# Seven products over 14 of 16 row tiles in the HGRN projections of a hybrid decoder step, with one weight sum on GpSimd

## The chip, the cores and the metric

The kernel runs on one core of a Trainium2 chip. The metric is the device time of one execution in microseconds (us). The kernel before takes 2852.39 us, the median of three runs (2851.09 to 2854.86).

## The reference

Two layers, the first RWKV-7, the second HGRN2, run over 512 prompt tokens and 8 x 4 sample tokens, 544 columns in all, with a model width of 2048. Everything is float32. The part that matters here is the input projection of the HGRN2 layer and the chunked recurrence that uses it:

```python
def hgrn2_mix(x, S_prev, lb, w_in, norm_w, w_o):
    q, f_logit, i, z = jnp.split(x @ w_in, 4, axis=-1)      # w_in: 2048 x 8192
    f = lb + (1.0 - lb) * jax.nn.sigmoid(f_logit)
    log_f = jnp.log(jnp.maximum(f, GATE_FLOOR))
    k = (1.0 - lb) * jax.nn.sigmoid(-f_logit)
    q = jax.nn.silu(q.astype(f32)) * HGRN_DK ** -0.5
    ...
    # per chunk: A = q k' with decays, o = A v + (q exp(G)) S, S = exp(G_last) S + k' v
    ...
    o = o * lax.rsqrt(jnp.mean(o * o, axis=-1, keepdims=True) + NORM_EPS) * norm_w
    out = (o.reshape(B, T, D).astype(x.dtype) * jax.nn.silu(z)) @ w_o
```

There are 16 heads of 128 channels; each head has four output tiles of 128 channels, for f, q, i (the values) and z (the gate).

## The kernel before

Activations are kept transposed: 16 row tiles (kt) of 128 channels by 544 tokens. A product in float32 accuracy is made of three TensorE passes over high and low parts: w_hi x_hi, w_hi x_lo and w_lo x_hi. ScalarE rounds a weight tile to its high part (a CAST), VectorE subtracts to get the low part. One pass over one half of the tokens is a matmul of 128x128 weights with 272 columns. A weight tile of 128 output channels, done plainly (function dense_kt), takes 16 row tiles x 2 token halves x 3 passes = 96 matmuls.

The HGRN tiles from number 20 to 75 are done in 28 pairs by a Strassen scheme with seven products in place of eight. A block is the pair's two output tiles times two row tiles times the two token halves. `U` counts the blocks along the rows. At U = 6 they take 12 of the 16 row tiles; the other 4 (`rest`, CW = 512 columns of the weight tile) are done plainly. One call of seven_products(q) is called a half here. It consists of eleven stretches, in this order: product 0, product 1, rest, rest, products 2, 3, 4, 5, rest, product 6, rest. A product is U x 3 matmuls, a rest is 4 x 3. After each three matmuls a counter goes up by one, and at certain counts a piece of the recurrence of the running or the last head is put between (`steps`): the level matmuls level(e, n) that build A, the outputs, the norm.

A head e from 1 to 14 has two halves: gates_pair (q even: it makes f and q of head e, and finishes head e-1) and values_pair (q odd: it makes v and z, and runs the levels of head e). Seven operands (items) of a half come from the two raw weight tiles raw[0] and raw[1]. Items 0, 1 and 6 are columns of the raw tiles. Items 2 to 5 are sums of them: S1 = raw1a + raw1b (weight_sum_1), S2 = S1 - raw0a (weight_sum_2), S3 = raw0a - raw1a (weight_sum_3), and S2 again = raw0b - S2 (weight_sum_4), which becomes item 5. All four sums stand on VectorE. Each item is then cast by ScalarE (item_hi) into one of three slots, and subtracted by VectorE (item_lo). VectorE also does the decays (widen), the copies of A (take), the states' chain (chain), the bank additions and the norms.

The order of the work on each engine is the order in which the code is written: gates_pair and values_pair exist once for ScalarE and once for VectorE, and the steps' counts set where TensorE does the recurrence. An engine does its list strictly in order, so an instruction that waits holds all that is behind it. The waits are:

- Level 0 waits for K and qr, level 1 for `first_q` (Q = qr * F, semaphore q1), and level n from 2 on for the widening before it (kx, qx).
- outputs(e, 0) waits for S[0] of `chain(e)`, outputs(e, 2) for S[2].
- The first matmul of product k waits for item_lo(q, k).
- GpSimd does the row sums of the activations once, before the pairs (row_sums), and then one product with the old sample states (t_Sd) and one masked copy (t_Vm) for each head.

Before the pairs, `scaled_rows`, `row_sums`, `sums_hi`, `sums_lo`, `third_sum_hi` and `third_sum_lo` make the seven combinations of the activations, once for each block j of the U.

Of the kernel before, what the change touches and what calls it, by code (L numbers as in the profile page):

```python
# [1392 lines left out]
def trunk(nc, keep, d):  # L1393

    with ExitStack() as ctx:
# [542 lines left out]
        def _(act):  # L1938
# [369 lines left out]
        def _(dve):  # L2308
# [18 lines left out]
            def weight_sum_1(q):  # L2327
                dve.wait_ge(raw_in[1], 16 * ((GS + 2 * q) // 2))
                if q:
                    dve.wait_ge(s.it_hi, ITEMS * (q - 1) + 4)  # L2330
                    dve.wait_ge(s.it_lo, ITEMS * (q - 1) + 4)
                dve.tensor_tensor(S1[:, :], raw[1][:, 0:UW], raw[1][:, UW:2 * UW], ALU.add).then_inc(s.s1, 1)

            def weight_sum_2(q):
                dve.wait_ge(raw_in[0], 16 * ((GS + 2 * q) // 2))
# [4 lines left out]
                else:  # L2340
                    dve.wait_ge(s.tile_ready, GS)
                dve.tensor_tensor(S2[:, :], S1[:, :], raw[0][:, 0:UW], ALU.subtract).then_inc(s.s2, 1)

            def weight_sum_3(q):
                if q:
                    dve.wait_ge(s.it_hi, ITEMS * (q - 1) + 5)
                    dve.wait_ge(s.it_lo, ITEMS * (q - 1) + 5)
# [513 lines left out]
```

## Time and profile before

| | us |
|---|---|
| median of three runs | 2852.39 |
| the profiled execution's own time | 2853.62 |
| its span, first to last instruction | 2851.8 |
| TensorE busy | 2730.1 (96%) |
| VectorE busy | 1608.9 (56%) |
| ScalarE busy | 1259.1 (44%) |
| GpSimd busy | 138.4 (5%) |

The page names engines PE (TensorE matmuls), PEld (its weight loads), DVE (VectorE), ACT (ScalarE), POOL (GpSimd) and SP (which issues DMAs). The pairs run from 1747.9 to 2562.8 us of the span. One head with its two halves takes 58.3 us. Matmuls are pipelined, so their recorded durations overlap: the time that one costs is the distance between starts. Durations of VectorE instructions overlap a little too.

### The profile page before, as it was taken

The page shows a single profiled execution, that of the slowest core. Times are in us where ns is not written, and L with a number is a line of the kernel's source. Part 1 is how long each engine was busy: PE and PEld are TensorE (multiplying, and loading weights), DVE is VectorE, ACT ScalarE, POOL GpSimd, SP SyncE. Part 2 cuts the span into 40 slices and gives each one's busy share as a digit, 9 for nine tenths or more (in the row PEclk, how much of TensorE's full clock was granted, in tenths as well). Part 3 has the DMA queues.
Part 4 walks back from the last instruction along what each step waited for, and adds up shares of the span by engine and source line. Part 5 has one row for each costly group of instructions (what it writes and reads, how often), then busy time and mean ns, then how long its engine had stood idle before and what let it go on. Part 6 is the DMA issues. An engine that isn't in the chain of part 4 may idle for free. (4 is left out here: it accounts for less than half of the span.)

```text
span 2851.8 us, 82517 instructions
## 1 busy us (share of the span) xinstructions
PE 2730.1 (96%) x36816; PEld 2567.6 (90%) x36816; DVE 1608.9 (56%) x2679; ACT 1259.1 (44%) x1869; POOL 138.4 (5%) x116
## 2 busy tenths in 40 slices
PE   6999999999999999999889988999999999999997
PEld 5899999999998887888779978999999999999997
DVE  7335313313326777888742267776777767775224
ACT  5345323324414555555532255444544455444222
POOL 0000000000001111010000003000000000000000
PEclk8999999999999999999999999999999999999999
DMA  3333333333311111112132242222333223243322
GB/s 126 108 106 113 109 113 113 113 111 134 115 69 52 50 53 54 51 53 71 43 111 89 90 155 73 95 95 94 97 100 107 95 80 114 95 139 137 124 89 102
DMA packets 86816, 273.48 MB, mean 96 GB/s; under 512 B 16448, under 2 KB 29504, under 8 KB 65984
## 3 DMA queue, kind: packets, MB, share of 16 engines
q1 hardware_dynamic: 77248, 250.37, 26.5%
q10 hardware_dynamic: 9216, 17.83, 1.7%
q8 instruction: 292, 4.78, 0.7%
q14 instruction: 60, 0.49, 0.1%
HBM read 221.63 MB, written 46.54 MB: 94 GB/s over the span
## 5 line engine op out<-in xcount | busy, mean ns | idle before, releaser
L136 PE MATMUL w_pair<-a_x_hi,keep_w_hi 128*128 128x272 f32 x2016 | 428.4, 294 | 19.3 <-DVE a_x_lo L1059 18.5
L136 PE MATMUL w_pair<-a_x_lo,keep_w_hi 128*128 128x272 f32 x2016 | 419.7, 289 | 0.0
L136 PE MATMUL w_pair<-a_x_hi,keep_w_lo 128*128 128x272 f32 x2016 | 417.4, 288 | 0.0
L1045 DVE TENSOR_TENSOR keep_w_lo<-keep_raw,keep_w_hi 128x2048 fp32r<-128x2048 f32 x63 | 144.4, 2293 | 469.5 <-ACT keep_w_hi L798 469.5
L136 PEld LDWEIGHTS w_pair<-a_x_hi,keep_w_hi 128*128 128x128 f32 x2016 | 320.2, 189 | 25.7 <-issue 20.7
L136 PEld LDWEIGHTS w_pair<-a_x_lo,keep_w_hi 128*128 128x128 f32 x2016 | 318.1, 189 | 0.0
L136 PEld LDWEIGHTS w_pair<-a_x_hi,keep_w_lo 128*128 128x128 f32 x2016 | 317.8, 189 | 0.0
L136 PE MATMUL t_pair<-t_x_hi,keep_w_hi 128*128 128x272 f32 x1216 | 262.0, 297 | 18.2 <-DVE t_x_lo L2421 9.1
L136 PE MATMUL t_pair<-t_x_lo,keep_w_hi 128*128 128x272 f32 x1216 | 253.5, 290 | 0.0
L136 PE MATMUL t_pair<-t_x_hi,keep_w_lo 128*128 128x272 f32 x1216 | 253.3, 290 | 0.0
L812 ACT ACTIVATE a_stage<-w_pair 128x544 f32<-128x544 f32 x64 | 40.0, 625 | 425.1 <-PE w_pair L136 425.1
L136 PEld LDWEIGHTS t_pair<-t_x_hi,keep_w_hi 128*128 128x128 f32 x1216 | 192.3, 190 | 27.8 <-issue 11.8
L1657 PE MATMUL t_pair<-t_x_hi,u_it_hi 128*128 128x272 f32 x672 | 201.4, 300 | 0.0
L136 PEld LDWEIGHTS t_pair<-t_x_lo,keep_w_hi 128*128 128x128 f32 x1216 | 194.2, 191 | 0.0
L1657 PE MATMUL t_pair<-t_x_hi,u_it_lo 128*128 128x272 f32 x672 | 193.5, 288 | 0.0
L1657 PE MATMUL t_pair<-t_x_lo,u_it_hi 128*128 128x272 f32 x672 | 193.5, 288 | 0.0
L136 PEld LDWEIGHTS t_pair<-t_x_hi,keep_w_lo 128*128 128x128 f32 x1216 | 192.5, 190 | 0.0
L1657 PE MATMUL t_pair<-u_To,u_it_hi 128*128 128x272 f32 x896 | 185.5, 300 | 0.0
L1657 PEld LDWEIGHTS t_pair<-u_To,u_it_hi 128*128 128x128 f32 x896 | 140.6, 189 | 13.8 <-issue 10.6
L1657 PE MATMUL t_pair<-t_x_hi,u_c_hi 128*128 128x272 f32 x448 | 137.2, 306 | 0.0
L2314 DVE TENSOR_TENSOR keep_w_lo<-keep_raw,keep_w_hi 128x2048 fp32r<-128x2048 f32 x38 | 87.7, 2307 | 84.4 <-ACT keep_w_hi L1948 84.4
L798 ACT CAST keep_w_hi<-keep_raw 128x2048 fp32r<-128x2048 f32 x63 | 120.2, 1908 | 30.5 <-ACT a_stage L812 28.0
(448 smaller groups left out, 6146.7 us busy)
## 6 DMA issues: line engine op xcount, KB each, us to landing
keep_raw<-in_w_in SPq DMA_DIRECT2D x64, 1024.0 KB, 5.0
keep_raw<-in_hgrn_in SPq DMA_DIRECT2D x64, 1024.0 KB, 5.1
keep_raw<-in_rwkv_wo SPq DMA_DIRECT2D x16, 1024.0 KB, 5.0
keep_raw<-in_hgrn_wo SPq DMA_DIRECT2D x16, 1024.0 KB, 5.0
t_Ss<-in_hgrn_s SPq DMA_DIRECT2D x16, 512.0 KB, 7.1
out_hgrn_s<-t_Sd SPq DMA_DIRECT2D x16, 512.0 KB, 8.5
scr_r<-a_stage ACTq DMA_DIRECT2D x16, 272.0 KB, 2.2
scr_k<-a_stage ACTq DMA_DIRECT2D x16, 272.0 KB, 2.1
```

The lines of the kernel that those rows point to most:

```text
L136: mm = pe.matmul(out[:, a, 0:TH], w, x[:, kt, a * TH:(a + 1) * TH], start=(kt == order[0] and n == 0), stop=(kt == order[-1] and n == 2))
L798: act.copy(w_hi[2 if n == 2 else n % 2][:, :], raw[n % 2][:, :]).then_inc(p.raw_hi, 1)
L812: act.activation(halves(stage[n % 2][:, :]), pair[3 if n == 2 else n % 2][:, :, 0:TH], func).then_inc(p.evac, 1)
L1045: dve.tensor_tensor(w_lo[b][:, :], raw[n % 2][:, :], w_hi[b][:, :].bitcast(F32), ALU.subtract).then_inc(p.raw_lo, 1)
L1657: mm = pe.matmul(out, a, b, start=start and m == 0, stop=(m == 2), skip_group_check=True)
L2314: dve.tensor_tensor(w_lo[g % 2][:, :], raw[g % 2][:, :], w_hi[g % 2][:, :].bitcast(F32), ALU.subtract).then_inc(s.raw_lo, 1)
```

## The change

- U goes from 6 to 7, so the seven products cover 14 of 16 row tiles: items are 896 columns wide and no longer 768, and the rest is 256 columns and no longer 512. A block j = 6 is added to the sums made before the pairs.
- S1 has no tile of its own: weight_sum_1 writes over raw1a. weight_sum_3, which reads raw1a, therefore has to come first, and the order of the sums is 3, 1, 2, one behind the other. In values_pair they stand together before first_q; at the end of values_pair they stand together for the next half.
- weight_sum_4 goes from VectorE to GpSimd, which does it for both halves of a head before the head's t_Sd.
- ScalarE's k_copy(e-1) comes before item_hi(q, 2) in gates_pair.
- TensorE's wait for t_lo moves from before product 0 to before product 2 of the first half; the last item has another slot, with a wait for it_lo before it; a few tiles are laid elsewhere.

```diff
-U = 6
+U = 7
...
+        S1 = raw[1][:, 0:UW]
...
                 if q == 0:
                     pe.wait_ge(s.evac, GS - 1)
-                    pe.wait_ge(s.t_lo, 2 * U)
...
+                if q == 0:
+                    pe.wait_ge(s.t_lo, 2 * U)
                 product(2, X, False)
...
# ScalarE
             def gates_pair(e, q):
+                if e > 1:
+                    k_copy(e - 1)
                 item_hi(q, 2)
                 if e > 1:
                     act.wait_ge(s.evac, H0 + 4 * e)
                     act.wait_ge(s.q1s, q)
                     silu(zs, s.zs)
-                    k_copy(e - 1)
...
                 if e == 0:
                     sums_hi(4)
                     sums_hi(5)
+                    scaled_rows(6)
...
                 k_copy(e)
                 if e < KT - 1:
-                    for j in range(U):
+                    for j in range(U - 1):
                         third_sum_hi(j)
+                    sums_hi(U - 1)
+                    third_sum_hi(U - 1)
# GpSimd
+            def weight_sum_4(q):
+                pool.wait_ge(s.it_hi, ITEMS * q + 3)
+                pool.wait_ge(s.it_lo, ITEMS * q + 3)
+                pool.tensor_tensor(S2[:, :], raw[0][:, UW:2 * UW], S2[:, :], ALU.subtract).then_inc(s.s4, 1)
...
             for e in range(KT):
+                if 1 <= e < KT - 1:
+                    weight_sum_4(2 * e - 2)
+                    weight_sum_4(2 * e - 1)
# VectorE
+            def weight_sum_1(q):
+                dve.wait_ge(s.s3, q + 1)
+                dve.tensor_tensor(S1, S1, raw[1][:, UW:2 * UW], ALU.add).then_inc(s.s1, 1)
...
             def gates_pair(e, q):
                 if q:
                     lower_first(q - 1, zs)
-                weight_sum_3(q)
                 item_lo(q, 2)
-                weight_sum_4(q)
                 item_lo(q, 3)
                 if e > 1:
                     chain(e - 1)
...
             def values_pair(e, q):
                 lower_first(q - 1, qr)
+                weight_sum_3(q)
                 weight_sum_1(q)
+                weight_sum_2(q)
                 first_q(e)
-                weight_sum_2(q)
                 item_lo(q, 2)
                 item_lo(q, 3)
                 take(e, 0)
                 widen(e, 0)
-                weight_sum_3(q)
-                weight_sum_4(q)
                 item_lo(q, 4)
...
                 lower_second(q, zs)
                 if q < NQ - 1:
+                    weight_sum_3(q + 1)
                     weight_sum_1(q + 1)
                     weight_sum_2(q + 1)
```

First, the order of VectorE at the start of an odd half, before. t_wS1 is S1, u3_wS2 is S2, u3_wS3 is S3, it_lo and it_hi are an item's parts, and t_Q<-t_qr,t_F is first_q.

```order
L2382 TENSOR_TENSOR t_qr<-t_pair0,t_rstd2 128x272
L2332 TENSOR_TENSOR t_wS1<-keep_raw1 128x768
L2478 TENSOR_TENSOR t_Q<-t_qr,t_F 128x544
L2342 TENSOR_TENSOR u3_wS2_22008<-t_wS1,keep_raw0 128x768
L2320 TENSOR_TENSOR u0_it_lo_22003<-u3_wS2_22008,u0_it_hi_22002 128x768
L2320 TENSOR_TENSOR u2_it_lo_22005<-t_wS1,u2_it_hi_22004 128x768
```

The same place in the changed kernel, where keep_raw1<-keep_raw1 is S1 written in place:

```order
L2396 TENSOR_TENSOR t_qr<-t_pair0,t_rstd2 128x272
L2356 TENSOR_TENSOR u3_wS3_22009<-keep_raw0,keep_raw1 128x896
L2360 TENSOR_TENSOR keep_raw1<-keep_raw1 128x896
L2367 TENSOR_TENSOR u3_wS2_22008<-keep_raw1,keep_raw0 128x896
L2492 TENSOR_TENSOR t_Q<-t_qr,t_F 128x544
L2341 TENSOR_TENSOR u0_it_lo_22003<-u3_wS2_22008,u0_it_hi_22002 128x896
L2341 TENSOR_TENSOR u2_it_lo_22005<-keep_raw1,u2_it_hi_22004 128x896
```

first_q had one sum ahead of it and now has three.

Second, VectorE around the start of an even half, before; t_S0 to t_S3 are the chain of the last head.

```order
L2378 TENSOR_TENSOR t_zs<-t_zs,t_rstd2 128x272
L2332 TENSOR_TENSOR t_wS1<-keep_raw1 128x768
L2342 TENSOR_TENSOR u3_wS2_22008<-t_wS1,keep_raw0 128x768
L2382 TENSOR_TENSOR t_zs<-t_pair0,t_rstd2 128x272
L2348 TENSOR_TENSOR u3_wS3_22009<-keep_raw0,keep_raw1 128x768
L2320 TENSOR_TENSOR u2_it_lo_22005<-u3_wS2_22008,u2_it_hi_22004 128x768
L2353 TENSOR_TENSOR u3_wS2_22008<-keep_raw0,u3_wS2_22008 128x768
L2320 TENSOR_TENSOR u1_it_lo_22007<-t_wS1,u1_it_hi_22006 128x768
L2526 COPY t_S0<-t_tok 128x128
```

And the same place in the changed kernel:

```order
L2392 TENSOR_TENSOR t_zs<-t_zs,t_rstd2 128x272
L2356 TENSOR_TENSOR u3_wS3_22009<-keep_raw0,keep_raw1 128x896
L2360 TENSOR_TENSOR keep_raw1<-keep_raw1 128x896
L2367 TENSOR_TENSOR u3_wS2_22008<-keep_raw1,keep_raw0 128x896
L2396 TENSOR_TENSOR t_zs<-t_pair0,t_rstd2 128x272
L2341 TENSOR_TENSOR u2_it_lo_22005<-u3_wS2_22008,u2_it_hi_22004 128x896
L2341 TENSOR_TENSOR u1_it_lo_22007<-keep_raw1,u1_it_hi_22006 128x896
L2542 COPY t_S0<-t_tok 128x128
```

Sum 3 is now ahead of sum 2, and sum 4 is gone from between the two low parts.

Third, GpSimd over one head in the changed kernel; before, only the second and third rows stood there.

```order
L2307 TENSOR_TENSOR u3_wS2_22008<-keep_raw0,u3_wS2_22008 128x896 x2
L2319 TENSOR_TENSOR t_Sd<-t_Ss,t_E4 128x1024
L2324 TENSOR_TENSOR t_Vm<-t_vtok,t_k_h_seq 64x512
```

The two sums of weights are one for each half of the head.

## Rows read from the trace of the kernel before

**Rows 1.** The page, busy time by engine: us (share of the span) x instructions.
```profile
PE 2730.1 (96%) x36816; PEld 2567.6 (90%) x36816; DVE 1608.9 (56%) x2679; ACT 1259.1 (44%) x1869; POOL 138.4 (5%) x116
```
**Rows 2.** PE's waits, 1747 to 2582 us: us in total, times, longest.
```profile
PE t_tok L1818 <- ACT t_ktok L2098: 1.5, 1, 1.5
PE t_lev L1828 <- DVE t_S L2526: 1.1, 1, 1.1
PE t_pair L136 <- DVE t_zs L2382: 0.6, 1, 0.6
```
**Rows 3.** The chain in order of time: start, us, what, matmuls.
```profile
1999.12 14.72 PE t_pair L1657 x117
```
**Rows 4.** Busy time in one odd and one even half.
```profile
2009.54:2037.44 27.90, 27.90 (x407) 25.97 (x405) 25.94 (x56) 12.82 (x24) 2.19 (x2) 1.00 0.34 118
2037.44:2067.87 30.43, 30.29 (x232) 28.25 (x231) 17.84 (x28) 16.26 (x26) 1.22 (x1) 1.00 0.26 79
```
**Rows 5.** DVE, timeline of the odd half: start, us, instruction.
```profile
2011.30 0.43 DVE L2382 TENSOR_TENSOR t_qr<-t_pair,t_rstd 128x272 f32<-128x272 f32 x1
2011.65 0.95 DVE L2332 TENSOR_TENSOR t_wS<-keep_raw 128x768 f32<-128x768 f32 x1
2012.51 0.72 DVE L2478 TENSOR_TENSOR t_Q<-t_qr,t_F 128x544 f32<-128x544 f32 x1
...
2016.02 0.96 DVE L2320 TENSOR_TENSOR u_it_lo<-t_wS,u_it_hi 128x768 fp32r<-128x768 f32 x1
...
2017.54 0.42 DVE L2500 TENSOR_TENSOR t_Q<-t_Q,t_F 128x272 f32<-128x272 f32 x1
```
**Rows 6.** PE, timeline of the odd half: levels 1 and 2.
```profile
2015.53 0.46 PE L1777 MATMUL t_lev<-t_Q,t_K 128*32 128x32 f32 x32
...
2019.93 0.46 PE L1777 MATMUL t_lev<-t_Q,t_K 128*32 128x32 f32 x32
```
**Rows 7.** DVE, timeline around the start of the even half at 2037.44.
```profile
2036.82 0.95 DVE L2332 TENSOR_TENSOR t_wS<-keep_raw 128x768 f32<-128x768 f32 x1
2037.86 1.62 DVE L2342 TENSOR_TENSOR u_wS<-t_wS,keep_raw 128x768 f32<-128x768 f32 x1
...
2040.62 0.95 DVE L2320 TENSOR_TENSOR u_it_lo<-u_wS,u_it_hi 128x768 fp32r<-128x768 f32 x1
...
2042.58 0.96 DVE L2320 TENSOR_TENSOR u_it_lo<-t_wS,u_it_hi 128x768 fp32r<-128x768 f32 x1
2043.46 0.28 DVE L2526 COPY t_S<-t_tok 128x128 f32<-128x128 f32 x1
```
**Rows 8.** ACT, the same place.
```profile
2039.51 0.83 ACT L1960 CAST u_it_hi<-u_wS 128x768 fp32r<-128x768 f32 x1 [2.45 <-DVE u_wS L2342]
2040.25 0.65 ACT L2068 ACTIVATE t_zs<-t_zs 128x544 f32<-128x544 f32 x1
...
2041.71 0.84 ACT L1960 CAST u_it_hi<-t_wS 128x768 fp32r<-128x768 f32 x1
```
**Rows 9.** PE, the same half: the outputs of the last head.
```profile
2044.45 0.61 PE L1828 MATMUL t_lev<-t_A,t_vtok 128*128 128x128 f32 x4
```
**Rows 10.** POOL's timeline, one head.
```profile
2022.33 1.90 POOL L2298 TENSOR_TENSOR t_Sd<-t_Ss,t_E 128x1024 f32<-128x1024 f32 x1 [41.98 <-DVE t_E L2502]
2037.14 1.52 POOL L2303 TENSOR_TENSOR t_Vm<-t_vtok,t_k_h_seq 64x512 f32<-64x512 f32 x1 [12.92 <-ACT t_vtok L2093]
```
**Rows 11.** DVE, two instructions of one form in that head.
```profile
2022.53 2.24 DVE L2324 TENSOR_TENSOR u_c_lo<-keep_raw,u_c_hi 128x512 fp32r<-128x512 f32 x1
...
2029.86 0.69 DVE L2324 TENSOR_TENSOR u_c_lo<-keep_raw,u_c_hi 128x512 fp32r<-128x512 f32 x1
```
**Rows 12.** L2303 and L2284 by themselves: ns min/median/max, first and last start.
```profile
L2303 POOL TENSOR_TENSOR t_Vm<-t_vtok,t_k_h_seq x16: 1033/1522/1747, 1756.0 to 2623.1; 64x512 f32<-64x512 f32 x16
...
L2284 POOL TENSOR_TENSOR t_Ss<-t_zs,t_acc x2: 771/772/772, 1700.2 to 1724.4; 128x272 f32<-128x272 f32 x2
```
**Rows 13.** PE's waits before the pairs, 1703 to 1748 us.
```profile
PE t_lev L1785 <- DVE t_Q L2500: 2.8, 1, 2.8
```
**Rows 14.** Busy time behind the wait of 2.8 us; PEclk is the granted clock's share.
```profile
1735.50:1739.40 3.90, 3.61 (x28) 3.31 (x28) 3.90 (x9) 0.59 (x2) 2.00 (x2) 0.56 0.00 0
```

More of the change, by code:

```diff
@@ L1403, in trunk @@
         raw, w_hi, w_lo, o = keep.raw, keep.w_hi, keep.w_lo, keep.o
-        acc, rstd, rstd2, warm = sb("acc", [P, T]), sb("rstd", [P, T]), sb("rstd2", [P, T]), sb("warm", [P, 1])
+        acc, rstd_at = sb("acc", [P, T]), nc.sbuf_base
+        rstd, rstd2, warm = sb("rstd", [P, T]), sb("rstd2", [P, T]), sb("warm", [P, 1])
         lb, oml = sb("lb", [P, KT]), sb("oml", [P, KT])
@@ L1409, in trunk @@
         vtok, ktok = sb("vtok", [P, 5, P]), sb("ktok", [P, 5, P])
+        S_at = nc.sbuf_base
         S = [sb(f"S{c}", [P, P]) for c in range(4)]
@@ L1423, in trunk @@
         Tl = Area(nc, "u7", keep.lora_at).sb("Tl", [P, 2, 2, TH], F32R)
-        T42 = [Tl[:, 0:2], To[:, 0:2], To[:, 2:4], To[:, 4:6], To[:, 6:8], To[:, 9:11]]
-        T1 = [To[:, i] for i in (12, 13, 14, 15, 8, 11)]
+        Tm, Tr = sb("Tm", [P, 2, 2, TH], F32R), Area(nc, "u8", rstd_at).sb("Tr", [P, 2, TH], F32R)
+        T42 = [Tl[:, 0:2], To[:, 0:2], To[:, 2:4], To[:, 4:6], To[:, 6:8], To[:, 9:11], To[:, 12:14]]
+        T1 = [Tr, To[:, 14], To[:, 15], To[:, 8], To[:, 11], Tm[:, 0], Tm[:, 1]]
         T3_raw = [t[:, :, :].rearrange("p b v -> p (b v)")[:, TH * i:TH * i + TH] for t in (Ss, Sd) for i in range(3)]
+        T3_raw.append(Area(nc, "u9", S_at).sb("T3s", [P, TH])[:, :])
         squares = [sq, rs]
@@ L1468, in item_source @@
         def item_source(k):
-            return (raw[0][:, 0:UW], raw[0][:, UW:2 * UW], S2[:, :], S1[:, :], S3[:, :], S2[:, :], raw[1][:, UW:2 * UW])[k]
+            return (raw[0][:, 0:UW], raw[0][:, UW:2 * UW], S2[:, :], S1, S3[:, :], S2[:, :], raw[1][:, UW:2 * UW])[k]
         def weight_tile(g):
@@ L1959, in item_hi @@
                     act.wait_ge(s.tile_ready, GS - 1 if n < 2 else GS)
+                if (q, k) == (NQ - 1, ITEMS - 1):
+                    act.wait_ge(s.it_lo, n)
                 act.copy(item_slot(q, k)[0][:, :], item_source(k)).then_inc(s.it_hi, 1)
@@ L1991, in sums_hi @@
                 act.wait_ge(s.t_sum, 4 * j + 4)
+                if j in (3, 4):
+                    act.wait_ge(s.t_in, 2 * j + 4)
                 act.copy(T1[j][:, 0], even[:, half(0)]).then_inc(s.t_hi, 1)
@@ L2325, in rest_lo, with weight_sum_3 @@
                                   ).then_inc(s.c_lo, 1)
-            def weight_sum_1(q):
+            def weight_sum_3(q):
+                dve.wait_ge(raw_in[0], 16 * ((GS + 2 * q) // 2))
                 dve.wait_ge(raw_in[1], 16 * ((GS + 2 * q) // 2))
                 if q:
-                    dve.wait_ge(s.it_hi, ITEMS * (q - 1) + 4)
-                    dve.wait_ge(s.it_lo, ITEMS * (q - 1) + 4)
-                dve.tensor_tensor(S1[:, :], raw[1][:, 0:UW], raw[1][:, UW:2 * UW], ALU.add).then_inc(s.s1, 1)
+                    dve.wait_ge(s.it_hi, ITEMS * (q - 1) + 5)
+                    dve.wait_ge(s.it_lo, ITEMS * (q - 1) + 5)
+                else:
+                    dve.wait_ge(s.tile_ready, GS)
+                dve.tensor_tensor(S3[:, :], raw[0][:, 0:UW], S1, ALU.subtract).then_inc(s.s3, 1)
+            def weight_sum_1(q):
+                dve.wait_ge(s.s3, q + 1)
+                dve.tensor_tensor(S1, S1, raw[1][:, UW:2 * UW], ALU.add).then_inc(s.s1, 1)
             def weight_sum_2(q):
-                dve.wait_ge(raw_in[0], 16 * ((GS + 2 * q) // 2))
                 dve.wait_ge(s.s1, q + 1)
@@ L2339, in weight_sum_2 @@
                     dve.wait_ge(s.it_lo, ITEMS * (q - 1) + 6)
[L2340 to L2347, printed above, removed]
-                dve.tensor_tensor(S3[:, :], raw[0][:, 0:UW], raw[1][:, 0:UW], ALU.subtract).then_inc(s.s3, 1)
-            def weight_sum_4(q):
-                dve.wait_ge(s.it_hi, ITEMS * q + 3)
-                dve.wait_ge(s.it_lo, ITEMS * q + 3)
-                dve.tensor_tensor(S2[:, :], raw[0][:, UW:2 * UW], S2[:, :], ALU.subtract).then_inc(s.s4, 1)
+                dve.tensor_tensor(S2[:, :], S1, raw[0][:, 0:UW], ALU.subtract).then_inc(s.s2, 1)
             def upper_first(q, t):
@@ L2525, in chain @@
                     dve.wait_ge(s.s_out, 16 * e)
+                else:
+                    dve.wait_ge(s.t3_lo, U)
                 dve.tensor_copy(S[0][:, :], blk(tok_ps, 0)).then_inc(s.S, 1)
@@ L2675, in _ @@
                     sums_lo(5)
-                    for j in range(U):
+                    for j in range(U - 1):
                         third_sum_lo(j)
+                    sums_lo(U - 1)
+                    third_sum_lo(U - 1)
                     chain(e)
                     scaled_out(n + 3, zs)
+                    weight_sum_3(0)
+                    weight_sum_1(0)
                     weight_sum_2(0)
```

6 lines of the change are left out of this document (2 added, 4 removed).

## Prediction

> **What bounds the kernel now.** I read the page first, for the engines' shares: PE is busy for 96% of the span, DVE for 56%, POOL for 5% [rows 1]. Then the list of PE's waits over the pairs: in 835 us PE waits three times, for 3.2 us in all [rows 2]. So a head's 58.3 us are matmuls end to end, and a matmul taken out is worth its full distance to the next one. Next I laid the table of one odd and one even half beside it. In the odd half DVE is busy for 25.9 of 27.9 us, in the even half for 17.8 of 30.4 [rows 4]. The 56% of the page hide this: in the odd half DVE is all but full, and what is put ahead of something PE needs there arrives later by its whole length. Last I read the timelines of DVE, ACT and PE at the two places where the order of DVE changes, for the room that each wait of PE has now.
>
> **What the change takes out.** A half has 7 x 18 + 4 x 12 = 174 matmuls of this kind, with U = 7 it has 7 x 21 + 4 x 6 = 171. That is 3 for each of 28 halves, 84 in all. One costs 0.124 us: a run of 117 covers 14.72 us, and (14.72 - 0.29) / 116 = 0.124, with the last one's 0.29 taken off [rows 3]. The gain is 84 x 0.124 = **10.5 us**, 0.75 us a head, if nothing else waits.
>
> **DVE's work and its lengths.** 544 elements take 0.72 us and 768 take 0.95 [rows 5], so 1.03 ns for one more, and an instruction of 896 takes 0.95 + 0.13 = 1.08 us. Instructions that don't depend on each other start 0.08 us before the last one's end. A dependent one starts 0.09 us behind it (2036.82 + 0.95 = 2037.77, the next at 2037.86 [rows 7]). So the new row of sums 3, 1, 2, each waiting for the one before, takes 1.17 us a piece. DVE's total falls (two sums leave a head, the rest is narrower), which is worth nothing by itself: only the order counts.
>
> **Level 1, in the odd half.** Now lower_first starts at 2011.30, one sum and first_q follow, first_q ends at 2012.51 + 0.72 = 2013.23 [rows 5], and PE reads it at 2015.53 [rows 6]: room of 2.3 us. Afterwards lower_first starts about 0.23 later (three wider low parts before it at +0.13, a wider cast, less 0.27 for the narrower rest). Then come three sums: first_q starts at 2011.88 + 1.17 + 1.17 + 1.00 = 2015.22 and ends at 2015.94. PE wants it 3 matmuls (0.37 us) earlier than now, since the even half is shorter: at 2015.15. With 0.14 us from DVE to PE, PE waits 0.9 us. For 14 heads that is **+13 us**; bounds 0.6 to 1.2 each.
>
> **Level 2, in the odd half.** It needs the first widening. The Q of it now ends at 2017.54 + 0.42 = 2017.96 [rows 5] and is read at 2019.93 [rows 6]. Afterwards sum 2 ends at 2015.30, its cast at 2016.27, its low part at 2017.38. At that moment GpSimd may start sum 4 and DVE the next low part. Rows show what happens then: while POOL's t_Sd ran from 2022.33 to 2024.23 [rows 10], a DVE subtraction begun at 2022.53 took 2.24 us, and the same form takes 0.69 elsewhere [rows 11]; it was done 0.54 us after POOL's end, as if begun 0.15 before that end. The other way round, POOL's t_Vm takes 1.52 beside DVE's sum, against 1.03 at the shortest [rows 10, 12]. So each holds the other for its whole length when both read two operands from SBUF.
>
> The Trainium skill says the same of the cause in "SBUF — State Buffer", "Who interferes with whom": a DVE instruction with two SBUF inputs contends with a GpSimd instruction that reads SBUF, and the second one blocks until the first is done. By this rule sum 4 gives DVE nothing back; by the view that an engine's work is its own, moving it would free 0.95 us twice a head. The trace agrees with the rule.
>
> How long sum 4 takes on GpSimd no row shows. Two true streams of 272 elements take 0.77 us [rows 12], 1024 with one broadcast operand 1.90 [rows 10]. The line through these gives 1.70 for 896; by 0.77 x 896 / 272 it would be 2.5 at most. I take 1.8, near the row of 1024. ("GPSIMD Engine Reference", "Performance versus the Vector engine", in the Trainium skill measured 4497 ns for 2048 elements; by proportion an estimate of 2.0 us, and the sum below would grow by some 5 us.)
>
> If DVE comes first, low part 3 ends at 2018.5, sum 4 at 2020.2, and the widening starts at 2020.05. If GpSimd comes first, sum 4 ends at 2019.3, low part 3 at 2020.2, and the widening starts behind the copies of A at 2020.4. Its K and Q parts (0.42 each [rows 5]) end 0.8 later, at 2020.8 or 2021.2. PE, already 0.9 late, wants it at 2019.56 + 0.93 = 2020.5. It waits 0.35 to 1.1 us; I take 0.7, for 14 heads **+10 us**. Products 4 to 6 then come late enough: the sum's work on DVE is behind, and the rest's low part is half as long.
>
> **The outputs, in the even half.** They need the chain's first state. Now S0 ends at 2043.46 + 0.28 = 2043.74 [rows 7] and is read at 2044.45 [rows 9], 7.01 us after the half begins, with 0.7 us of room. Afterwards, counted from the half's begin: the three sums start at -0.1 (now -0.6; the half's last casts and low parts are wider, PE's side shorter). t_Vm falls on them and adds 0.7, as it makes a sum of 0.95 into 1.62 today [rows 7]. They end at -0.1 + 3.5 + 0.7 = 4.1. The cast takes 0.94 (0.83 for 768 [rows 8] plus 128 elements at 0.85 ns), low part 2 1.08: 6.2. GpSimd now starts sum 4 surely first, since the cast of item 3 comes behind the silu and a bank copy (it starts 2.2 us after the cast of item 2 today [rows 8], some 1.7 after the k copies have left) and ends at 6.7. Sum 4 runs to 8.0; low part 3 lets the chain start at 8.8, S0 is there at 9.1, and PE reads at 9.25 in place of 7.0. PE waits 2.2 to 2.6 us; I take 2.4, for the 13 heads that have a chain there **+31 us**. The k copies ahead of the cast cost nothing there and bring kv forward by up to 0.1 us: -1 us.
>
> **Before the pairs.** A seventh block adds two ACT passes of 544 (0.65 each, as the silu in [rows 8]) ahead of the key copy, for which PE waits 1.5 us already, at 1747 us [rows 2]: +1.3. The seventh block's four sums on POOL (0.77 each [rows 12]), casts and low parts then stand before the first chain, and three sums in place of one behind it, before product 2 of the first half, which t_lo now guards too. Today there is room of some us; I take +3.5 more, between 0 and 6. Together **+5 us**.
>
> **Sum.** -10.5 + 13 + 10 + 31 - 1 + 5 = +47.5. On the profiled execution (2853.6, of which 2851.8 is span) this gives 2901; on the median of the runs, which is 1.2 below it, **2900 us**. PE's wait times shift all that follows equally, because the norm of the even half, from which ACT and DVE start their long row to level 1, is itself a step of PE: no head catches up. I leave DMA out: a raw tile is asked for when sum 4 and the low parts are done, as now, and PE's late steps give it more time and not less.
>
> **Rivals.**
> - The waits fall into room, and the change is *faster*: DVE idles in a third of the even half [rows 4], and if DVE's row before first_q and before S0 were released earlier than I think, only the 10.5 us and the 1.3 us ahead of the key copy would count: 2843. It decides at 2.3 us of delay for first_q and 0.7 for S0. My rows give 2.7 and 3 or more, and the row of DVE has no idle time in it at level 1, so little speaks for it: 0.08.
> - GpSimd and DVE don't hold each other in this sum (both true streams, other addresses). Then level 2 costs nothing and the outputs wait 1.3: -10.5 + 13 + 13 x 1.3 - 1 + 5 = +23, 2876. [Rows 11] speak against it: 0.15.
> - The clock falls. The longest wait before, 2.8 us [rows 13], is followed by a stretch with a granted clock of 0.56, so mostly at 1.2 GHz and not 2.4, over about 3.4 us [rows 14]. The wait of 1.5 us [rows 2] brought none that the page shows. A wait of 2.4 each head lies between; if each brought such a stretch, at up to 1.5 us: 13 x 1.5 = +20, 2920. Chance 0.15.
> - Room that I didn't see takes half of each wait, and the time stays: -10.5 + 26 / 2 - 1 = about 2854. Chance 0.05.
> - The forecast, 2885 to 2912: 0.57.
>
> **Numbers.** The range of 2866 to 2922 holds the forecast, the rival without holding and the one with the clock. 0.2%, about 6 us, is what a measurement of this kernel can tell from no change. Faster by more: 0.08; within it: 0.05; slower by more: 0.87.
>
> **What the new profile would show.** L1657's successor has 4788 matmuls and not 4872. PE's waits over the pairs show t_lev waiting for DVE's t_Q some 28 times (0.9 and 0.7 us) and t_lev's outputs waiting for t_S 13 times (2.4 us). A head takes 61.5 and not 58.3 us. Sum 4 on POOL takes 1.7 to 2.1 us, and low part 3 beside it takes over 2. If the outputs don't wait, the largest term is wrong and the time is under 2875.

## The result and the profile after

The changed kernel takes 2920.49 us (median of four runs, 2919.98 to 2921.87); the kernel before, run beside it, took 2852.86 (2851.09 to 2854.86). The ratio is 1.0244 with a 95% interval of 1.0230 to 1.0258. It is slower, as forecast, but by 68 us and not by 47.5. The profiled execution has a span of 2920.1 us.

The page's line of engines after the change. DVE has gained 47 us and POOL 80 against [rows 1]. PE's busy time went up by 7 us, so 61 of the 68 us that the span grew by are idle time of PE. But the change took 84 matmuls out, 10.5 us, so PE is busy some 18 us longer than its work explains; the rows at the end of this section show why.
```profile
PE 2737.3 (94%) x36732; PEld 2573.3 (88%) x36732; DVE 1656.4 (57%) x2654; ACT 1268.4 (43%) x1874; POOL 218.0 (7%) x148
```
PE's waits over the pairs, 1747 to 2640 us (us in total, times, longest), which answer to [rows 2]. Where 3.2 us stood there are now 61. The wait of 1.1 us before the last head's outputs, which is in [rows 2], lies at 2642 us now and so behind this window.
```profile
PE t_lev L1833 <- DVE t_S L2542: 36.2, 13, 2.8
PE t_lev L1782 <- DVE t_K L2512: 11.1, 14, 0.8
PE t_lev L1782 <- DVE t_Q L2492: 9.3, 14, 0.7
PE t_pair L1661 <- DVE u_it_lo L2341: 4.1, 1, 4.1
PE t_pair L136 <- DVE t_zs L2396: 0.6, 1, 0.6
```
From top to bottom: the outputs, level 2, level 1 and, once, product 2 of the first half. The last row stood in [rows 2] too.

DVE's timeline in an odd half (start, us, instruction; a wait in brackets), where [rows 5] stood. Three sums end right before first_q. Low parts 2 and 3 follow, and then the first K widening (L2512) takes 2.07 us, where its Q twin takes 0.43.
```profile
2167.45 1.08 DVE L2356 TENSOR_TENSOR u_wS<-keep_raw 128x896 f32<-128x896 f32 x1
2168.56 1.09 DVE L2360 TENSOR_TENSOR keep_raw<-keep_raw 128x896 f32<-128x896 f32 x1
2169.69 1.09 DVE L2367 TENSOR_TENSOR u_wS<-keep_raw 128x896 f32<-128x896 f32 x1
2170.70 0.72 DVE L2492 TENSOR_TENSOR t_Q<-t_qr,t_F 128x544 f32<-128x544 f32 x1
...
2172.91 1.09 DVE L2341 TENSOR_TENSOR u_it_lo<-keep_raw,u_it_hi 128x896 fp32r<-128x896 f32 x1
...
2174.22 2.07 DVE L2512 TENSOR_TENSOR t_K<-t_K,t_F 128x272 f32<-128x272 f32 x1
2176.21 0.43 DVE L2514 TENSOR_TENSOR t_Q<-t_Q,t_F 128x272 f32<-128x272 f32 x1
```
PE's levels 1 and 2 in that half, where [rows 6] stood.
```profile
2171.47 0.46 PE L1782 MATMUL t_lev<-t_Q,t_K 128*32 128x32 f32 x32 [0.68 <-DVE t_Q L2492]
...
2176.74 0.43 PE L1782 MATMUL t_lev<-t_Q,t_K 128*32 128x32 f32 x29 [0.79 <-DVE t_K L2512]
```
POOL over the same head, where [rows 10] stood. Sum 4 takes 2.96 us in the odd half and 2.08 in the even one.
```profile
2173.02 2.96 POOL L2307 TENSOR_TENSOR u_wS<-keep_raw,u_wS 128x896 f32<-128x896 f32 x1 [34.29 <-DVE u_it_lo L2341]
...
2193.88 1.91 POOL L2324 TENSOR_TENSOR t_Vm<-t_vtok,t_k_h_seq 64x512 f32<-64x512 f32 x1 [12.71 <-ACT t_vtok L2102]
2200.11 2.08 POOL L2307 TENSOR_TENSOR u_wS<-keep_raw,u_wS 128x896 f32<-128x896 f32 x1 [4.32 <-DVE u_it_lo L2341]
```
Put side by side, these two timelines show the holding in both orders. In the odd half POOL's sum starts at 2173.02 beside DVE's low part 3 (2172.91 to 2174.00): it runs 0.9 us longer, to 2175.98, and the K widening that starts at 2174.22 is done only at 2176.29. In the even half (below) POOL is first, and low part 3 pays.

DVE around the start of the even half, where [rows 7] stood: the second sum takes 1.81 beside POOL's t_Vm, low part 3 takes 2.58 beside sum 4, and S0 (L2542) is there at 2203.33.
```profile
2194.93 1.81 DVE L2360 TENSOR_TENSOR keep_raw<-keep_raw 128x896 f32<-128x896 f32 x1
2196.78 1.09 DVE L2367 TENSOR_TENSOR u_wS<-keep_raw 128x896 f32<-128x896 f32 x1
...
2198.87 1.09 DVE L2341 TENSOR_TENSOR u_it_lo<-u_wS,u_it_hi 128x896 fp32r<-128x896 f32 x1 [0.66 <-ACT u_it_hi L1967]
2200.55 2.58 DVE L2341 TENSOR_TENSOR u_it_lo<-keep_raw,u_it_hi 128x896 fp32r<-128x896 f32 x1 [0.59 <-ACT u_it_hi L1967]
2203.05 0.28 DVE L2542 COPY t_S<-t_tok 128x128 f32<-128x128 f32 x1
```
PE's outputs in the same half, where [rows 9] stood.
```profile
2203.48 0.68 PE L1833 MATMUL t_lev<-t_A,t_vtok 128*128 128x128 f32 x4 [2.78 <-DVE t_S L2542]
```
Last, what the list of waits doesn't show. Four windows of the trace (stretch, length, busy times, then PEclk, the granted clock; DMA share; GB/s), the kind of view of [rows 14]: behind the first output wait shown, behind another one, behind the third, and behind the wait of 4.1 us.
```profile
1886.90:1890.30 3.40, 3.40 (x29) 3.40 (x29) 1.98 (x5) 1.69 (x3) 0.00 (x0) 1.00 0.73 282
1949.90:1953.40 3.50, 3.50 (x19) 3.50 (x18) 1.43 (x2) 1.53 (x3) 0.00 (x0) 0.51 0.51 213
2203.50:2206.90 3.40, 3.40 (x29) 3.40 (x29) 1.98 (x5) 1.70 (x3) 0.00 (x0) 1.00 0.65 270
1758.80:1775.90 17.10, 14.60 (x57) 12.53 (x57) 8.30 (x9) 7.04 (x11) 4.07 (x2) 0.50 0.18 61
```
The three output waits are equally long (2.8 us), the clock behind them is not: 29 matmuls pass in one stretch of 3.4 us, 19 in the other, at 1.2 GHz in place of 2.4. The trace has such stretches behind 8 of the 13 output waits, six of 3.4 us and two of 6.8, and the distance from one head's outputs to the next tells what they cost. It is 61.86 us where the clock stays, and 63.1 to 64.7 behind outputs where it falls (before: 58.32). The excess adds up to 14.5 us (1.6 + 2.8 + 1.3 + 1.6 + 1.6 + 2.8 + 1.3, and 1.5 for the last fall). Behind the wait of 4.1 us the clock is low for 17 us: from the first outputs to the second it is 72.44 us, and with the waits alone it would be 65.95 (58.34 - 0.75 + 0.66 + 0.79 + 2.77 + 4.14), so 6.5 us more are the clock's.

Behind the pairs it is the other way round. The trace of the kernel before has a stretch of 6.8 us at half clock at 2637 us that the changed kernel's trace lacks at the same place. First the kernel before, then the changed one:
```profile
2636.70:2643.50 6.80, 6.80 (x25) 5.04 (x25) 3.44 (x6) 2.07 (x3) 0.00 (x0) 0.50 0.46 189
```
```profile
2708.30:2715.10 6.80, 6.80 (x48) 5.84 (x48) 3.83 (x6) 2.04 (x3) 0.00 (x0) 1.00 0.48 193
```
From the last head's outputs to the end of the span it is 280.65 us before and 277.40 after, so 3.3 us of the clock's cost are not in the difference.

### The profile page after: what moved, and what is told of

It reads as the page before. It is cut to its first block and busy times, and to the rows that moved or that the text cites. A ratio compares the mean times of both kernels' runs of the same rounds, so it can differ in the third digit from the quotient of the medians.

```text
span 2920.1 us, 82337 instructions
## 1 busy us (share of the span) xinstructions
PE 2737.3 (94%) x36732; PEld 2573.3 (88%) x36732; DVE 1656.4 (57%) x2654; ACT 1268.4 (43%) x1874; POOL 218.0 (7%) x148
## 5 line engine op out<-in xcount | busy, mean ns | idle before, releaser
L1045 DVE TENSOR_TENSOR keep_w_lo<-keep_raw,keep_w_hi 128x2048 fp32r<-128x2048 f32 x63 | 144.4, 2293 | 469.7 <-ACT keep_w_hi L798 469.7
L1661 PE MATMUL t_pair<-t_x_hi,u_it_hi 128*128 128x272 f32 x784 | 235.6, 301 | 0.0
L1661 PE MATMUL t_pair<-t_x_lo,u_it_hi 128*128 128x272 f32 x784 | 226.4, 289 | 0.0
L1661 PE MATMUL t_pair<-t_x_hi,u_it_lo 128*128 128x272 f32 x784 | 226.3, 289 | 0.0
L136 PEld LDWEIGHTS t_pair<-t_x_hi,keep_w_hi 128*128 128x128 f32 x1216 | 191.4, 189 | 27.5 <-issue 11.1
L2341 DVE TENSOR_TENSOR u_it_lo<-keep_raw,u_it_hi 128x896 fp32r<-128x896 f32 x112 | 141.5, 1263 | 55.7 <-ACT u_it_hi L1967 55.2
L1661 PEld LDWEIGHTS t_pair<-t_x_hi,u_it_hi 128*128 128x128 f32 x784 | 148.1, 189 | 4.9 <-issue 2.6
L1661 PEld LDWEIGHTS t_pair<-t_x_lo,u_it_hi 128*128 128x128 f32 x784 | 148.4, 189 | 0.0
```

What stands on the lines that cost most here:

```text
L136: mm = pe.matmul(out[:, a, 0:TH], w, x[:, kt, a * TH:(a + 1) * TH], start=(kt == order[0] and n == 0), stop=(kt == order[-1] and n == 2))
L1045: dve.tensor_tensor(w_lo[b][:, :], raw[n % 2][:, :], w_hi[b][:, :].bitcast(F32), ALU.subtract).then_inc(p.raw_lo, 1)
L1661: mm = pe.matmul(out, a, b, start=start and m == 0, stop=(m == 2), skip_group_check=True)
L2341: dve.tensor_tensor(lo[:, :], item_source(k), hi[:, :].bitcast(F32), ALU.subtract).then_inc(s.it_lo, 1)
```

## The experiments

Each was run beside the kernel before on the same chip; its median there was 2846.3 to 2850.8 us. "Head" is the distance between the outputs of two successive heads, read from the traces.

| kernel | median, us | ratio to before (95%) | head, us |
|---|---|---|---|
| changed kernel | 2920.49 | 1.0244 (1.0230 to 1.0258) | 61.86 to 64.7 |
| e1, matmuls in the output wait | 2906.87 | 1.0200 (1.0182 to 1.0219) | 61.84 |
| e2, chain first | 2867.01 | 1.0068 (1.0049 to 1.0087) | 58.86 |
| e3, sum 4 on VectorE | 2898.95 | 1.0177 (1.0161 to 1.0192) | 61.67, twice 60.1 |
| e4, GpSimd's sum later | 2886.99 | 1.0128 (1.0109 to 1.0148) | 60.37 |
| e11, e3 with matmuls in the wait | 2881.63 | 1.0118 (1.0099 to 1.0137) | 60.04 |
| e5, before with sum 4 on GpSimd | 2869.49 | 1.0084 (1.0070 to 1.0097) | 60.01 |
| e6, before with the new order | 2860.69 | 1.0054 (1.0041 to 1.0068) | 59.3 |
| e7, e2 with sum 4 on VectorE | 2855.14 | 1.0020 (1.0010 to 1.0031) | 58.02 |
| e8, e7 with product 1 earlier | 2846.61 | 0.9986 (0.9976 to 0.9995) | 57.48 |
| e9, e8 with a shorter way into the pairs | 2841.75 | 0.9972 (0.9960 to 0.9983) | 57.48 |
| e10, e9 with affine steps on ScalarE | 2836.66 | 0.9950 (0.9930 to 0.9970) | 57.20 |

The experiments ran in four groups, and the median of the kernel before differs between them: 2850.84 us beside e1 to e4, 2849.48 beside e7 to e10, 2846.30 beside e5 and e6, 2848.64 beside e11, and 2852.86 beside the changed kernel. So a difference between medians of two groups is uncertain by a few us. Each set against its own kernel before, e1 regains 11.6 us of the change's loss (13.6 by the medians), e2 51.5 (53.5), and e11 regains 15.1 against e3 (17.3). The distances between heads, read from one trace each, have no such doubt.

**e1: is it the clock?** Eleven matmuls that nothing reads are put into the output wait of 13 heads.
```diff
                 if c0 == 0:
                     pe.wait_ge(s.a_ev, 7 * e + 7)
+                    if 1 <= e <= KT - 3:
+                        for _ in range(11):
+                            pe.matmul(lev_ps[0][:, 0:TH], x_hi[:, 0, 0:P], x_hi[:, 0, 0:TH], start=True, stop=True)
                     pe.wait_ge(s.S, 4 * e + 1)
```


> The changed kernel, with 11 matmuls of 272 columns put on PE ahead of its wait for S0 (heads 1 to 13), into a PSUM bank that the outputs overwrite: a part of the computation is not changed, the extra products are thrown away. They take 1.4 us of the 2.8 us in which PE idles there, so PE's wait still ends with S0. Theory A (the time over my sum is the clock, which falls to half behind idle times of 2.8 us): the low stretches between 1900 and 2600 us go, about 13 us, 2907 us; the outputs wait 1.4 us idle in place of 2.8, and the low stretch of 17 us at 1759 stays. Rival B (the clock falls for another reason, such as the wait for product 2 or the power drawn): low stretches stay, 2920 us.

Measured 2906.87. PE's timeline at one wait, the added matmuls and the outputs:
```profile
1882.87 1.54 PE L1831 MATMUL t_lev<-t_x_hi 128*128 128x272 f32 x11
1885.76 0.71 PE L1836 MATMUL t_lev<-t_A,t_vtok 128*128 128x128 f32 x4 [1.35 <-DVE t_S L2545]
```
Within a head the outputs start no earlier, since S0 comes no earlier, yet the kernel is 13.6 us faster by the medians. All low stretches in the heads are gone, and every head takes 61.84 us. From the second head's outputs to the last head's it is 802.8 us in place of 817.7, so the clock's share there is 14.8 us, which agrees with the 14.5 added up above. (Of this, 3 us are lost again in e1's trace: it has the stretch of 6.8 us at half clock behind the pairs that the kernel before has and the changed kernel lacks.) The idle stretch of 1.35 us that is left brings no fall.

**e2: the chain.** In gates_pair the chain goes ahead of low parts 2 and 3.
```diff
-                item_lo(q, 2)
-                item_lo(q, 3)
                 if e > 1:
                     chain(e - 1)
+                item_lo(q, 2)
+                item_lo(q, 3)
```


> The changed kernel, with chain(e-1) on DVE ahead of the low parts of items 2 and 3 in gates_pair. A: the outputs no longer wait (S0 is there 1.3 us before PE comes), 13 x 2.8 = 36 us go and the low clock with them (13 us): 2871 us. The waits of level 1 and 2 (0.66 and 0.79 us, 14 times) stay as they are. B (something else holds the outputs, the key sums kv or the copies of A): the wait stays over 2 us, 2920.

Measured 2867.01. One output wait of 1.1 us is left in the list (as in [rows 2]), levels 1 and 2 keep theirs:
```profile
PE t_lev L1782 <- DVE t_K L2512: 11.1, 14, 0.8
PE t_lev L1782 <- DVE t_Q L2492: 9.2, 14, 0.7
PE t_pair L1661 <- DVE u_it_lo L2341: 4.1, 1, 4.1
PE t_lev L1833 <- DVE t_S L2542: 1.1, 1, 1.1
```
The chain's first state, in the even half of one head, now has only the key product to wait for:
```profile
2108.81 0.29 DVE L2542 COPY t_S<-t_tok 128x128 f32<-128x128 f32 x1 [0.67 <-PE t_tok L1823]
```
The place of two lines was worth 53 us by the medians: a head is 3.0 us shorter than an undisturbed one of the changed kernel (39 us for 13 heads), and no head shows the lower clock, which is the rest. Low parts 2 and 3, put off by the chain's 1.4 us, are waited for by nobody.

**e3 and e11: sum 4 alone.** weight_sum_4 goes back to VectorE, at its places of before.
```diff
                 item_lo(q, 2)
+                weight_sum_4(q)
                 item_lo(q, 3)
 ...
                 widen(e, 0)
+                weight_sum_4(q)
                 item_lo(q, 4)
```


> The changed kernel, with weight_sum_4 back on VectorE: between low parts 2 and 3 in gates_pair, behind the first widening in values_pair. A (GpSimd's sum holds DVE for its whole length): level 2 no longer waits (-11 us), the outputs wait 1.8 and not 2.8 us (-13 us), and with the shorter idle time the clock falls less or not (0 to -14 us): 2882 to 2896 us, I say 2885. B (the sum on GpSimd is hidden, so putting it back adds 1.1 us of DVE twice a head): the outputs wait longer by 1.1 us and the time goes up to 2935.

Measured 2898.95, 14 us above that. The waits came out as the theory has it (level 2 none, outputs 25.0 us over 14), but the clock fell behind 11 of the 13 waits of 1.85 us. To test that this is the missing 14 us, e11 puts 8 matmuls into the wait of e3.

> The kernel in which the fourth weight sum is back on VectorE in the changed order (measured 2898.95 us, 14 us above what was expected of it), with 8 matmuls that nothing reads ahead of TensorE's wait for S0, in 13 heads; they shorten the idle stretch of 1.85 us to about 0.8 us and leave the head's other work where it was. Theory (the 14 us were the clock, which fell to half behind 11 of the 13 waits): no head shows the lower clock, the heads come every 60.1 us, 2880 us. Rival (the matmuls that follow these waits are slow for another reason, or the missing time is elsewhere in the head): 2895 us or more.

Measured 2881.63. The window behind the second head's outputs, in e3:
```profile
1880.00:1883.40 3.40, 3.40 (x16) 3.40 (x17) 1.06 (x4) 1.20 (x2) 0.00 (x0) 0.50 0.72 282
```
and in e11, with the idle stretch cut to 0.75 us:
```profile
1880.50:1883.90 3.40, 3.40 (x29) 3.40 (x29) 2.05 (x5) 1.72 (x3) 0.00 (x0) 1.00 0.70 277
```
A head takes 60.04 us, the figure of the two undisturbed heads of e3. The 17 us between e3 and e11 are the clock's: 11 stretches of 3.4 us at half speed, 1.6 us each. Without the clock in either, a head is 1.8 us shorter with the sum on VectorE than with it on GpSimd (60.04 against 61.86).

**e4: who holds whom in the even half.** GpSimd's sum waits until the chain is done.
```diff
                 if 1 <= e < KT - 1:
+                    if e > 1:
+                        pool.wait_ge(s.S, 4 * e)
                     weight_sum_4(2 * e - 2)
                     weight_sum_4(2 * e - 1)
```


> The changed kernel; GpSimd's sum 4 of the even halves waits for the end of chain(e-1), from head 2 on. Nothing on DVE is moved. A: low part 3 takes 1.1 and not 2.6 us, the outputs wait 1.3 and not 2.8 us (-19 us), idle times of 1.3 us don't let the clock fall (-13 us): 2888 us. B (low part 3 is long for another reason than GpSimd's sum): no change, 2920.

Measured 2886.99. DVE's low part 3 and S0, with POOL out of the way:
```profile
2184.24 1.09 DVE L2343 TENSOR_TENSOR u_it_lo<-keep_raw,u_it_hi 128x896 fp32r<-128x896 f32 x1 [0.58 <-ACT u_it_hi L1967]
2185.25 0.28 DVE L2544 COPY t_S<-t_tok 128x128 f32<-128x128 f32 x1
```
1.09 in place of 2.58: the 1.5 us of holding are 1.5 us of each output wait (2.8 to 1.3), and the clock stays up behind waits of 1.3.

**e5: the same sum in the kernel before.** U stays 6 and the old order stays, only the sum of the paired tiles moves.
```diff
+            def weight_sum_4(q):                       # GpSimd
+                pool.wait_ge(s.it_hi, ITEMS * q + 3)
+                pool.wait_ge(s.it_lo, ITEMS * q + 3)
+                pool.tensor_tensor(S2[:, :], raw[0][:, UW:2 * UW], S2[:, :], ALU.subtract).then_inc(s.s4, 1)
 ...
-                weight_sum_4(q)                        # VectorE, in gates_pair and in values_pair
```


> The kernel before the change, in which only the fourth weight sum of the paired tiles goes to GpSimd. Theory (GpSimd and VectorE hold each other up on shared SBUF operations, 2.08 to 2.96 us for the sum and about 2 us for a K widening beside it): no gain, 2859 us, with waits of 0.2 to 0.3 us before outputs or products in each half. Rival (the sum is hidden on an idle engine): 2852 us or less.

Measured 2869.49, a loss of 23 us against the kernel before beside it. The theory had 7, the rival none. POOL and DVE in an odd half, each from its own timeline:
```profile
1903.90 2.58 POOL L2294 TENSOR_TENSOR u_wS<-keep_raw,u_wS 128x768 f32<-128x768 f32 x1 [31.23 <-ACT u_it_hi L1960]
```
```profile
1904.99 1.79 DVE L2501 TENSOR_TENSOR t_K<-t_K,t_F 128x272 f32<-128x272 f32 x1
1906.70 0.43 DVE L2503 TENSOR_TENSOR t_Q<-t_Q,t_F 128x272 f32<-128x272 f32 x1
```
and PE's waits over the pairs:
```profile
PE t_lev L1777 <- DVE t_Q L2503: 10.8, 14, 0.8
PE t_lev L1777 <- issue: 3.3, 14, 0.3
```
The K widening is held for 1.4 us again. Level 2 has room for that and doesn't wait; the delay passes down DVE's list, and PE waits 0.3 before level 3 and 0.8 before level 4. What DVE was to gain in return, it doesn't: where sum 4 stood in the list, it now idles for a cast.
```profile
1909.26 0.96 DVE L2328 TENSOR_TENSOR u_it_lo<-u_wS,u_it_hi 128x768 fp32r<-128x768 f32 x1 [0.90 <-ACT u_it_hi L1960]
```
From the K widening to this low part it is 4.27 us, and 2.90 in the kernel before: later by the whole holding. A head is 1.7 us longer, of which the list of waits shows 1.0 to 1.1; the rest lies in gaps too short for it. I had priced only the products and the outputs. Moving 28 x 0.95 us of work to an engine that is 5% busy made the kernel slower by itself.

**e6: the new order in the kernel before.** Six products, sum 4 on VectorE, but the sums in the order 3, 1, 2 together.
```diff
                 lower_first(q - 1, qr)
+                weight_sum_3(q)
                 weight_sum_1(q)
-                first_q(e)
                 weight_sum_2(q)
+                first_q(e)
```


> The kernel before the change with six products and its sums on VectorE, but with the changed kernel's order: the sums 3, 1, 2 together ahead of first_q and at the end of the values. Theory (the order makes the chain late, the number of products does not): about 2860 us, with a wait of 0.6 us before outputs in each of 13 heads. Rival (the seventh product's missing matmuls leave VectorE short of time, not the order): 2852 us, no wait before outputs.

Measured 2860.69. That is the expected figure by luck only: the kernel before was at 2846.30 beside it, so the order costs 14.4 us, where the theory gave 8. The sign is right, the size and the place are not. PE waits before kv, the product of the keys with the values, and not before the outputs:
```profile
PE t_tok L1818 <- ACT t_ktok L2098: 13.8, 13, 1.1
```
ScalarE's timeline there: it waits 3.5 us for the late sums with a cast, and the key copies stand behind the cast.
```profile
2040.32 0.84 ACT L1960 CAST u_it_hi<-u_wS 128x768 fp32r<-128x768 f32 x1 [3.51 <-DVE u_wS L2342]
2041.06 0.65 ACT L2068 ACTIVATE t_zs<-t_zs 128x544 f32<-128x544 f32 x1
2041.62 0.56 ACT L2097 COPY t_ktok<-t_tok 128x512 f32<-128x512 f32 x1
```
The changed kernel has its key copies ahead of the casts, and no head of it waits before kv. So with the sums together that edit is probably worth about 1.1 us a head; no run takes it out of the changed kernel. I had priced it against the old order, at 0.1 us.

**e7 to e10: putting it right.** e7 is e2 with sum 4 on VectorE, behind low part 3 (even halves) and behind the first widening (odd halves).

> The changed kernel with the chain ahead of the low parts 2 and 3 and with the fourth weight sum back on VectorE. Theory (three causes: the held K beside GpSimd's sum, the late chain, the clock behind long waits): against the same order with the sum on GpSimd (2867 us) the level 2 wait of 11.1 us goes, at about 0.9 us of VectorE work in each half that has slack there; 2856 us. TensorE's output waits stay near zero and no head shows the lower clock. Rival (GpSimd's sum is off the path and the level 2 wait comes from VectorE's own order): 2867 to 2875 us, level 2 wait still 11 us.

Measured 2855.14, with no level 2 wait. Level 1 kept its 9.3 us. e8 takes product 1's high part ahead of the sigmoids and its low part ahead of the gate:
```diff
-                sigmoids(e)
                 item_hi(q + 1, 1)
+                sigmoids(e)
 ...
-                gate(e)
                 item_lo(q + 1, 1)
+                gate(e)
```


> The kernel of the previous entry, with the high and low part of the next head's product 1 taken ahead of the sigmoids (ScalarE) and of the gate (VectorE). Theory: the level 1 wait of 0.66 us a head, which ends on first_q, loses the 0.45 us by which first_q stands behind product 1's low part; -6 us, 2850 us. Rival: first_q only moves behind the gate and stays as late as it was; 2856 us.

Measured 2846.61; the level 1 wait in its list:
```profile
PE t_lev L1782 <- DVE t_Q L2489: 3.1, 14, 0.2
```
e9 then makes the way into the pairs shorter: weight_sum_3(0) right behind sums_lo(5), and GpSimd's t_Sd of head 0 behind the low part of the third product, number 2.

> The kernel of the previous entry, and ahead of the pairs: the third weight sum of the first pair stands right behind the sums of the last loaded tile, and GpSimd's S of head 0 waits for product 3's low part. Theory (a wait of 4.1 us before product 2 of the first half costs itself and a stretch of 17 us at half clock behind it, about 6.8 us): the wait falls to 1.2 us, the long stretch goes, 2841 us. Rival (the clock falls there whatever the wait is): only the 2.9 us go, 2847 us.

Measured 2841.75. The wait before product 2 is 1.5 us in place of 4.1, and the low stretch behind it 3.4 us in place of 17. From e8 to e9 the heads are the same to 0.01 us; the 4.9 us between the medians lie before them. (The first outputs come 2.9 us later and the second ones 4.5 earlier: 7.4 us less between them, 2.6 of it the wait, the rest the clock. The two edits were not run apart.) e10 gives the gate's two affine steps to ScalarE:
```diff
                 sigmoids(e)
+                act.wait_ge(s.sig, 2 * e + 2)
+                act.activation(F[:, :], F[:, :], ACT.Identity, scale=oml[:, e:e + 1], bias=lb[:, e:e + 1]).then_inc(s.f1, 1)
+                act.activation(K[:, :], K[:, :], ACT.Copy, scale=oml[:, e:e + 1]).then_inc(s.kg, 1)
```


> The kernel of the previous entry, with the gate's two affine steps on ScalarE and only the clamp on VectorE. Theory: VectorE is the engine that TensorE waits for at level 1, and 0.7 us less work ahead of first_q takes the rest of that wait; 2837 us, below the kernel before the change. Rival: ScalarE's two steps delay its copies of the products, and the wait comes back in front of the matmuls that reuse those banks; 2845 us or more.

Measured 2836.66. PE's waits over the pairs are back to three:
```profile
PE t_lev L1833 <- DVE t_S L2544: 1.1, 1, 1.1
PE t_pair L1661 <- DVE u_it_lo L2338: 0.8, 1, 0.8
PE t_pair L136 <- DVE t_zs L2398: 0.6, 1, 0.6
```
This version beats both kernels, by 0.3 to 0.7% the one before. The intervals of e8 and e9, and of e9 and e10, touch, so for these steps the distances in the traces say more than the medians. What seven products alone are worth isn't shown by it: the kernel before with six products was not run with the chain first, product 1 earlier and the affine steps on ScalarE. A head of 57.20 is 1.12 us shorter than before: 0.75 are the six matmuls; the distances between matmuls are shorter by 0.2 us at the seams, where one group of matmuls follows another, and by 0.1 in kv; the rest isn't assigned.

## Why the prediction was off by 20 us

| step | forecast, us | measured, us |
|---|---|---|
| 84 matmuls fewer | -10.5 | 4788 of them in the trace; -10.5 |
| level 1 | +13 | 9.3, and 14 heads |
| level 2 | +10 | 11.1, and 14 heads |
| outputs | +31 | 36.2, and 13 heads |
| key copies | -1 | not measured here; e6, which lacks them, waits 1.1 a head before kv |
| before the pairs | +5 | 4.1 + 0.7 of waits |
| clock | 0, a rival of +20 | 14.5 in the heads, 6.5 behind the wait of 4.1, -3.3 behind the pairs |

**Right.** The sign, and the place and count of every wait in the heads: t_Q at level 1 in 14 heads, the held widening at level 2 in 14, the chain's first state in 13. The holding between GpSimd and DVE, on which the second and third term rested ([rows 11]), is shown by e4 in the even half and by e5 and e7 in the odd half. It is what the Trainium skill says in "SBUF — State Buffer", "Who interferes with whom", for an instruction of VectorE with two SBUF inputs beside a GpSimd read, and this case's numbers agree in both orders of issue: DVE 1.09 to 2.58 when POOL is first, POOL 2.08 to 2.96 when DVE is first.

**The step that failed** is "The clock falls", which stood among the rivals at 0.15 and at nothing in the sum. The window in [rows 14] had shown it behind 2.8 us. I took my own output wait of 2.4 to lie between 2.8 and the harmless 1.5, and let it count as harmless; it then came out at 2.8, the very length of the row. e1 shows 14.8 us for it in the heads (13.6 by the medians), e11 17 us in a kernel whose waits are 1.85. So 2.4 lay between two lengths that both brought the fall, and counting it as harmless was wrong even for the wait that I forecast. The rival's mechanism was right and its size nearly so (20), but it is made up otherwise: 14.5 us behind 8 of 13 output waits, 6.5 us behind a wait that I hadn't weighed for the clock at all, since it stood inside a lump of +3.5 for the prologue, and 3.3 us that only the kernel before loses behind the pairs. (Of 17 us, 14.6 were busy at half speed, which makes 7 us at most; from e8 to e9 13.7 us less of it gave 4.8.) The net of 17.7 us is also what PE's busy time says: it rose by 7.2 us with 10.5 us of matmuls gone.

**Mis-sized terms.** Outputs: 2.8 and not 2.4, mostly because sum 4 takes 2.08 us on GpSimd in the even half and not 1.8. (The estimate of 2.0 from the Trainium skill's "GPSIMD Engine Reference", "Performance versus the Vector engine", was nearer than my line through the rows, whose longer one has a broadcast operand.) Level 1: 0.67 and not 0.9; that first_q's way is what I took it for is shown by e8, where moving one low part took 0.44 of it. Of the 0.24 us too many, 0.09 are the row of sums (3.25 us from sum 3's start to first_q's, and not 3.34) and 0.09 the way from DVE to PE (0.05 us there, and not 0.14). With level 2 and the prologue the errors nearly cancel, which is luck: -10.5 + 9.3 + 11.1 + 36.2 + 4.8 = +50.9, against +47.5. The clock's 14.5 + 6.5 - 3.3 = 17.7 bring it to 68.6, and the two spans differ by 68.3.

**Two slips in the rivals,** neither of which touches the forecast. Half of the waits of 13, 10 and 31 us is 27 and not 13, so the rival of the unseen room stands for about 2868 us and not for an unchanged 2854. And DVE idles in two fifths of the even half (12.6 of 30.4 us [rows 4]), not in a third.

**What stayed open.** Why equal output waits of 2.8 us bring the fall in 8 heads and not in 5. The falls begin between 0.8 us before and 1.2 us after PE is at work again, and in e3 they come in 11 heads of 13 behind shorter waits. They don't come at random. In e3 the fall begins 1.2 us behind the outputs' start, then 1.0, 0.8, 0.5, 0.3 and 0.1 in the heads that follow; the next head has none, and then it is 1.2 again. In the changed kernel the pattern repeats after seven heads: four falls (1.2, -0.8, -0.6 and 1.1 us behind the outputs' start), then three heads without. So it depends on when a wait comes and not on its length alone. Why, no run here tells.

## What to carry to other kernels

Price each new wait of TensorE in two parts: its own length, and the stretch at half clock that may follow; where a trace shows the fall behind a wait of the length you forecast, it belongs in the sum. An idle GpSimd is no free place for an elementwise sum of two SBUF operands while VectorE has work of that kind near its deadline: measure what VectorE does in the same microseconds. When work is regrouped on a full engine, order it by what TensorE needs next; here two lines moved in one place gave back some 51 to 53 of 68 us.

## What the runs showed of the hardware

- Idle stretches of TensorE of 1.3 to 1.4 us (13 heads each in e1 and e4) brought no fall of the granted clock, nor did one of 2.2 us before the pairs (changed kernel, 1746.6 us). Of 1.85 us, 11 of 13 did (e3), of 2.8 us, 8 of 13. While it is at half, matmuls of 272 columns start 0.23 us apart and not 0.125.
- The wait of 4.1 us before product 2 came with 17 us at half clock in the changed kernel, e2, e3, e7, e8 and e11; TensorE was busy for 14.6 of those 17 us in the changed kernel. With the wait at 2.8 (e1, e4) it was 13.7 us, and with 1.5 (e9) 3.4 us. But in e10 the wait was 0.8 and the clock was low for 10.2 us there, after 10 us at the full clock, so the length of this wait alone doesn't set it. Ahead of it, e10 had a wait of 2.7 us before kv with 3.4 us at half clock behind it.
- A GpSimd subtraction of 896 elements with two SBUF operands takes 2.08 us by itself, one of 768 takes 1.81. Beside VectorE work with two SBUF operands each side finishes about as late as if the later one had begun when the earlier one ended.
